# Half the gathered tokens in a PEER block: wider up products, high part first, gathers a batch ahead, GELU stores on ScalarE's queue

## What is computed

```python
q = (xt @ w_q).reshape(T, PEER_HEADS, 2, PEER_HALF)
s = jnp.einsum('thpc,hpnc->thpn', q, sub_keys)
s_top, i_top = lax.top_k(s, PEER_TOPK)
cand_s = s_top[:, :, 0, :, None] + s_top[:, :, 1, None, :]     # 16 x 16 sums
cand_i = i_top[:, :, 0, :, None] * N_KEYS + i_top[:, :, 1, None, :]
best_s, pos = lax.top_k(cand_s, PEER_TOPK)
idx = jnp.take_along_axis(cand_i, pos, axis=-1)
gate = jax.nn.softmax(best_s, axis=-1)
...
act = jax.nn.gelu(jnp.einsum('tkd,td->tk', u_tab[ib], xb), approximate=False)
return jnp.einsum('tk,tkd->td', act * gb, v_tab[ib])
```

## Time and profile before

| what | us |
|---|---|
| median of 3 runs | 1585.91 |
| lowest and highest run | 1579.07, 1590.8 |
| the profiled execution's own time | 1588.34 |
| its span, first to last instruction | 1586.6 |
| TensorE busy | 1471.9 |
| VectorE busy | 1274.1 |

### The profile page before, as it was taken

How to read it: one execution, slowest core, us unless ns; L and a number is a source line. 1 busy time by engine, 2 the same in 40 slices (tenths; PEclk the granted TensorE clock), 3 DMA queues, 4 the chain that set the end, 5 groups by cost and what they waited for, 6 DMA issues and landing times.

```text
span 1586.6 us, 25321 instructions
## 1 busy us (share of the span) xinstructions
PE 1471.9 (93%) x9438; PEld 1325.3 (84%) x9438; DVE 1274.1 (80%) x2444; ACT 824.7 (52%) x1571; POOL 506.2 (32%) x425
## 2 busy tenths in 40 slices
PE   7999799999989888888897888999989999999999
PEld 6898688789889888888897887889878888888887
DVE  4638787776798697877867876999989999999997
ACT  4553453151434656655665854554455556565553
POOL 4011620110466666656661111322322222222220
PEclk9999899999999999989999999999999999999999
DMA  6220004030465788887889998999899999999993
GB/s 201 81 81 1 8 29 162 28 125 35 143 209 181 270 289 285 282 269 259 286 285 394 369 353 307 379 379 372 328 414 410 410 410 409 407 411 405 409 401 124
DMA packets 168439, 420.49 MB, mean 265 GB/s; under 512 B 12896, under 2 KB 100096, under 8 KB 151680
## 3 DMA queue, kind: packets, MB, share of 16 engines
q1 hardware_dynamic: 140608, 251.10, 44.8%
q0 software_dynamic: 27712, 167.82, 27.1%
HBM read 372.44 MB, written 46.40 MB: 264 GB/s over the span
## 4 chain that ended last, share of the span: by engine, by line
PE 55%; DMA 7%; DVE 4%; issue 4%; POOL 3%; ACT 2%; SPq 1%; ACTq 0%; DVEq 0%
PE bank L2432 7%; PE bank L2434 7%; PE bank L2433 7%; PE bank L2108 5%; PE bank L2109 5%; PE bank L2110 5%; DMA early_gelus<-early_gelu 5%; PE bank L2127 4%; PE banks L2432 3%; PE banks L2434 3%; PE banks L2433 3%; POOL u_split L2008 2%; PE bank L2420 2%; PE bank L2421 2%; PE bank L2422 2%
## 5 line engine op out<-in xcount | busy, mean ns | idle before, releaser
L2108 PE MATMUL bank<-x_hi,u_split 128*128 128x320 f32 x832 | 268.7, 323 | 7.8 <-POOL u_split L2008 7.3
L2109 PE MATMUL bank<-x_lo,u_split 128*128 128x320 f32 x832 | 260.3, 313 | 0.0
L2110 PE MATMUL bank<-x_hi,u_split 128*128 128x320 f32 x832 | 259.8, 312 | 0.0
L1804 POOL DMA_INDIRECT scores<-in_peer_uv,pair_index x86 | 106.7, 1241 | 392.2 <-DVE pair_sum L1828 391.2
L2108 PEld LDWEIGHTS bank<-x_hi,u_split 128*128 128x128 f32 x832 | 160.7, 193 | 12.2 <-issue 9.8
L2479 ACT ACTIVATE act_tile<-onehots 128x384 f32<-128x384 f32 x128 | 124.3, 971 | 82.3 <-DVE act_lo L2521 76.9
L2127 PE MATMUL bank<-onehot_j,onehot_gated 128*128 128x128 f32 x768 | 109.2, 293 | 58.6 <-issue 42.0
L2109 PEld LDWEIGHTS bank<-x_lo,u_split 128*128 128x128 f32 x832 | 160.4, 193 | 0.0
L2110 PEld LDWEIGHTS bank<-x_hi,u_split 128*128 128x128 f32 x832 | 159.8, 192 | 0.0
L2127 PEld LDWEIGHTS bank<-onehot_j,onehot_gated 128*128 128x128 f32 x768 | 100.9, 204 | 65.8 <-issue 65.1
L2008 POOL TENSOR_TENSOR u_split<-u_raw,u_split 128x1024 fp32r<-128x1024 f32 x41 | 99.2, 2420 | 119.8 <-ACT u_split L2165 61.2
(11 more groups left out here) (433 smaller groups left out, 4037.0 us busy)
## 6 DMA issues: line engine op xcount, KB each, us to landing
v_raw<-in_peer_v SPq DMA_DIRECT2D x128, 512.0 KB, 10.7
u_raw<-in_peer_u SPq DMA_DIRECT2D x64, 512.0 KB, 5.5
u_raw_more<-in_peer_u SPq DMA_DIRECT2D x64, 512.0 KB, 4.9
gates<-gate_stage SPq DMA_DIRECT2D x24, 1024.0 KB, 11.6
onehots<-gates SPq DMA_DIRECT2D x32, 768.0 KB, 11.6
early_gelus<-early_gelu SPq DMA_DIRECT2D x104, 160.0 KB, 4.8
gelu_tile<-early_gelus SPq DMA_DIRECT2D x104, 160.0 KB, 11.3
w_raw<-in_w_in SPq DMA_DIRECT2D x9, 1024.0 KB, 5.0
```

Of the source, the lines that this page charges most:

```text
L1804: pool.indirect_dma_start(self.slot(k), None, self.table, bass.IndirectOffsetOnAxis(ap=self.sidx[:, k:k + 1], axis=0)).then_inc(self.lande ...
L2108: nc.tensor.matmul(out, uh[:, q, w], m.xh[:, k, P + NS:], start=(k == 0), stop=False)
L2109: nc.tensor.matmul(out, uh[:, q, w], m.xl[:, k, P + NS:], start=False, stop=False)
L2110: t = nc.tensor.matmul(out, ul[:, q, w], m.xh[:, k, P + NS:], start=False, stop=(k == KD - 1))
```

## The change

NS goes from 64 to 32, so TU from 320 to 352 columns, NR from 2 to 4, and the dots from 64 to 32. EARLY goes from 104 to 96, so iterations with an up product in the last stage from 24 to 32. With the new table ups_in, FIRST goes from 27 to 21; batches 0 to 31 hold 54 up products in place of 56 (10 batches with one, in place of 8), batches 32 to 47 hold 16 as before, and 5 follow. GpSimd fetches before the low parts, four rows in batch 0 and then two, so for the dots of the next batch. An up product waits for the high part, runs its 16 matmuls with it, and only then waits for the low part. ScalarE itself issues the GELU store, right behind the GELU, and waits for that GELU first. SyncE keeps the u loads (now 4 tiles ahead in its order, in place of 6) and the gate stores.

```diff
-EARLY = 104
+EARLY = 96
...
-NS = 64
+NS = 32
...
-    ups_in = [1 if n >= LATE or n % 4 == 3 else 2 for n in range(NB_)]
+    ups_in = [1 if n >= LATE or n % 3 == 2 else 2 for n in range(NB_)]
...
-                def store_gelu(n):
-                    banks.wait_taken(sp, ("up", n))
-                    sp.dma_start(gelus[n], ge[:, n % 2, 0:TU]).then_inc(nxt.ge_out[n % 2], 16)
-
...
                 for n in range(NB_):
                     for t in ups_of[n]:
-                        tile(t)
+                        load_u(t + NU)
                     if n % 2:
                         store_gates(n)
...
                 for n in range(LATE):
+                    for k in range(fetched, min(NS, fetched + (DOTS if n else 2 * DOTS))):
+                        up_rows.fetch(pool, k)
+                        fetched += 1
                     for t in ups_of[n]:
                         pool_low(t)
-                    for k in range(fetched, min(NS, fetched + DOTS)):
-                        up_rows.fetch(pool, k)
-                        fetched += 1
...
                     banks.wait_free(pe, g)
-                    wait_low(pe, n)
+                    pe.wait_ge(u_hi, n + 1)
                     q, out = n % 2, banks.bank(g)[:, 0:TU]
                     for k in range(KD):
                         w = slice(k * P, (k + 1) * P)
                         nc.tensor.matmul(out, uh[:, q, w], m.xh[:, k, P + NS:], start=(k == 0), stop=False)
                         nc.tensor.matmul(out, uh[:, q, w], m.xl[:, k, P + NS:], start=False, stop=False)
+                    wait_low(pe, n)
+                    for k in range(KD):
+                        w = slice(k * P, (k + 1) * P)
                         t = nc.tensor.matmul(out, ul[:, q, w], m.xh[:, k, P + NS:], start=False, stop=(k == KD - 1))
...
                     nc.scalar.activation(ge[:, n % 2, 0:TU], banks.bank(("up", n))[:, 0:TU],
                                          ACT.Gelu).then_inc(banks.taken["act"], 1)
+                    banks.wait_taken(act, ("up", n))
+                    act.dma_start(gelus[n], ge[:, n % 2, 0:TU]).then_inc(nxt.ge_out[n % 2], 16)
```

More of the change, by code:

```diff
@@ L2043, in store_gates @@
                                  stage[:, q].rearrange("p g t j -> p g (t j)")).then_inc(stored[q], 16)
-                def tile(n):
-                    if n + 6 < EARLY + NU:
-                        load_u(n + 6)
-                    store_gelu(n)
-                for n in range(2, 6):
+                for n in range(2, FIRST + NU):
                     load_u(n)
-                for n in range(FIRST):
-                    tile(n)
                 for n in range(NB_):
                     for t in ups_of[n]:
-                        tile(t)
+                        load_u(t + NU)
                     if n % 2:
@@ L2062, in _ @@
                             sp.dma_start(m.v_raw[i], v_rows[i]).then_inc(nxt.v_in[i], 16)
-                for n in range(EARLY - LAST, EARLY):
-                    tile(n)
+                for n in range(EARLY - LAST + NU, EARLY + NU):
+                    load_u(n)
                 for half in range(2):
```

## The result

| | us |
|---|---|
| before, median of 3 runs | 1585.91 (1579.07 to 1590.8) |
| changed, median of 3 runs | 1569.09 (1568.38 to 1569.77) |
| ratio, 95% interval | 0.9892 (0.9842 to 0.9941) |
| span of the changed kernel's profiled execution | 1567.4 |

The forecast was 1567, range 1550 to 1597. The change gains 1.1%, 16.8 us. By the prediction's stages the span moved from 1586.6 to 1567.4 so: A 14.7 shorter, B 43.4 shorter, C 3.7 shorter, D 42.6 longer.

A forecast was written before the change was run, and what follows sets the result against it. TensorE was taken as the bound in Stage D, with gather waits in Stage B and VectorE or bandwidth in Stage C. 901.9 + 665.9 = 1567.8 of span, plus 1.74 outside, less 2.43, gave 1567 us, range 1550 to 1597.

The forecast's parts named there:

- Stage A: Up products alone, to the first gate product's end: forecast to end at 509.3, where before it was 521.3.
- GpSimd's hold: Batch 0: four gathers, the fourth waiting for dot 3 at 503.5, delay a low part to 507.0.
- Stage B: Batches 0 to 31, 310.8 us before: forecast 259.6 of TensorE work plus 13 of gaps, ending at 781.9.
- 9 or 10 more: First 14 batches: VectorE 0.7 us a batch slower than TensorE, partly overlapping late low parts, 13 us in all.
- Stage C: Batches 32 to 47 and five last up products, 128.5 us before: forecast 120, bounds 112 and 130.
- Stage D: The last stage, bound by TensorE, 626.0 us before: forecast 39.9 longer, 665.9.
- The 1.5 us set aside for 1% more bytes: Last stage, iterations without an up product: 16 KB more GELU loads, between nothing and 3.5 us.
- The first: Rival: bandwidth holds batches 32 to 47 at 128.5 us, stores or u loads still waiting; 1582 us, chance 0.15.
- The second: Rival: gathers still late in 14 batches, low parts behind them, 28 to 32 us more; 1597 us, chance 0.08.
- The third: Rival: long DMA issues on ScalarE's queue hold its other work, 23.3 us; 1599 us, chance 0.10.
- The fourth: Rival, better: gaps in batches 0 to 31 near 3 us, the next stage near 113; 1551 us, chance 0.09.
- The 41 us of TensorE's work: Whole kernel: 352 columns in place of 320 make each of 128 up products 0.32 us longer.

The follow-up runs named there:

- e4: The changed kernel with GpSimd's gathers put back behind the low parts of their batch, two per batch: 1587.64 us.
- e8: The changed kernel with SyncE's u loads two tiles further ahead, so a load stands in front of its batch's gate store: 1565.68 us.
- e11: e9 with the GELU stores on ScalarE's queue and SyncE's u loads two tiles further ahead, so all three reorderings at 64 tokens: 1530.41 us.
- e2: The changed kernel with the GELU stores back on SyncE's queue and the u loads in their old order: 1577.53 us.
- e1: The changed kernel run again with no edit, as the standard for the runs beside it: 1569.28 us.
- e7: The kernel before with the GELU stores on ScalarE's queue and the u loads in the new order: 1598.82 us.
- e6: The kernel before (64 tokens, 104 early tiles) with the gathers a batch ahead, four in batch 0, and nothing else: 1560.62 us.
- e9: e6 with the high part first, GELU stores still on SyncE: 1546.12 us.
- e3: The changed kernel with each up product waiting for the low part before its first matmul: 1572.61 us.
- e10: The kernel before with the new numbers (32 tokens, 96 early tiles, new table) and the gathers ahead, low parts first, stores on SyncE: 1574.25 us.

## Why the prediction was right, point by point

**Stage A, GpSimd's hold at 509.3: right, but forecast 2.7 us too late.** (The prediction's own terms, 507.0 + 1.28 + 0.89, add up to 509.2.) The hold is where the prediction put it. "VectorE's selection does not change and delivers onehot_j at 507.0" is the part that failed: onehot_j was done at 501.9, dot 3 at 498.5 in place of 503.5. The likely reason was not in the account: VectorE stalls while GpSimd makes a low part (below), and in the changed kernel these stalls add up to some 8 us where before has 13. No run tried it apart. Half of the 5 us was lost again, since behind the 6.91 us of idle time the 8 low matmuls took 504.69 - 502.17 = 2.52 in place of 1.28, and gate product 1 1.91 in place of 0.89: the lower level of the clock, 1.2 GHz (mean granted clock 0.60 from 500 to 510 us).

**Stage B, 259.6 of work and 13 of gaps: right in kind, forecast 5.2 too long.** The gaps were 267.4 - 259.6 = 7.8, inside the bounds of 3 and 45. The low parts were priced right: two were expected late with some 5 us, three were, with 5.4. The term that failed is the "9 or 10 more" for VectorE. It was level, as the prediction has it, busy for 117.17 of the 118 us from 507 to 625, about the 14 batches with dots. But that is some 8.4 us a batch and not 8.8, TensorE's waits in that stretch are the 5.4 us for low parts alone, and behind it TensorE has none. e4 shows that the gathers' place in GpSimd's order carries the stage: 21.2 us of it.

**Stage C, 120: forecast 4.8 too short.** The term that failed is "A u load now stands right behind a gate store [...] so I give it nothing". Issues of 12.00 and 13.09 us made it 19.7 us of waits. e8 takes them away, and C gives back 1.9 to 2.8 of the 4.8, because the gate stores are late instead; with 64 tokens and the loads sooner C is 120.1 (e11). What was right: the stores' own waits went (41.1 to 2.6), at a price of 0.33 and 0.40 us of ScalarE's time per tile. e2 puts the stores' move, with the u loads' new place that goes with it, at 8.3 us, of which 4.2 in C; the stores alone are 11.9, of which 7.0 in C (e2 against e8).

The Trainium skill ("DMA: Bandwidth & Descriptors", section "Issuing engines are not separate DMA queues") holds that a second issuing engine saves only the sequencer's time to initiate the transfer, and that this is usually small beside the transfer. Taken as the prediction took it, C would have stayed at 128.5. It was 124.8, and 129.9 with the stores back on SyncE (e2), at DMA shares of 1.05 and 1.04. The measurement decides against that forecast. It bears the rule out in that the transfers themselves took nearly as long as before and what was saved was time ahead of the issue; but here that time was not small, 2.8 to 2.9 us a store in the median, beside some 7 us to landing. The rule that each DMA engine goes round its queues packet by packet (same page, "Queues, rings and completion order") is neither shown nor refuted: a store landed in 7.1 us from SyncE's queue and in 7.2 and 5.8 from ScalarE's.

**Stage D, 665.9: forecast 2.7 too short.** The 38.4 us of wider and more up products were right. The 1.5 us set aside for 1% more bytes was the wrong account of the 4.2 that followed. Counted by the starts of the down product's matmuls from 1250 to 1480 us, one comes every 0.2303 us in each of the nine kernels of 32 tokens and every 0.2287 in each of the five of 64, at a granted clock of 1.00. Over the 128 x 18 matmuls of the down products that is 3.7 us, an estimate that takes them all alike. The pause behind the last up products is 5.46 us in place of 4.43, another 1.0. Neither the DMA (e1's last stretch) nor the reorderings (every kernel of a width has the same pace) are why. The cause stays open; where the buffers lie in memory, which the width also moves, was not tried.

**The sum.** The errors, measured less forecast, are -2.7, -5.2, +4.8 and +2.7: 1567.8 of span against 1567.4. The total was better than its parts, and that is luck: two stages were forecast too long and two too short by nearly the same. The 2 us between 1567 and the measured median of 1569.09 come from taking off 2.43 for a profiled execution above its median; the changed kernel's profiled execution is its median.

**The rivals.** The first (bandwidth holds C) fell with 41.1 to 2.6 us of store waits, though its second half, the u loads behind the gate stores, took place. The second (gathers still late) fell: VectorE has no such wait in the list for B. The third (ScalarE held by its queue) fell as told: no issue of a GELU store there was over 0.35 us. But e7 shows a form of it that the prediction didn't have: not a long issue, but 0.75 us of ScalarE per tile, which fits a loss of up to 14 us when ScalarE lies on the path of B and none when it doesn't. The fourth (better) was met in B only.

**What the prediction didn't ask.** It weighed the change as one. Gathers ahead are 23.5 us alone (e6) and 18.4 in the whole (e4); stores on ScalarE's queue are a loss of 12 to 15 alone (e7) and a gain of 11.9 (e2 against e8) and 15.7 (e9 against e11) behind the gathers; the high part first is 14.5 at 64 tokens (e9) and 3.3 at 32, which is not clear of the noise (e3); the new numbers cost 3.2 alone, 13.6 behind the gathers (e10), and 35.3 behind all reorderings (e8 against e11). The 41 us of TensorE's work were right in the sum; that they bought waits which a reordering takes away for nothing was not looked at.

## What to carry to other kernels

A change that pays with work on the bound engine for fewer waits elsewhere should be priced against the kernel whose waits have first been taken away by reordering: here the trade was nearly even alone and cost 35 us afterwards. In an in-order queue, put what another engine needs a step later ahead of what waits, and then look who stands behind it. Take a combined change apart before keeping it whole, since the same step can lose 12 us or gain 12 by what else is in place.

## What the runs showed of the hardware

VectorE stood still while GpSimd worked. In before, two neighbouring instructions of VectorE on 128x128 values, and the low part that GpSimd ran meanwhile:

```profile
428.74 0.23 DVE L1455 CAST packed_words<-packed 128x128 uint32<-128x128 f32 x1
429.00 2.44 DVE L1456 TENSOR_SCALAR packed_low<-packed_words 128x128 uint32<-128x128 uint32 x1
```

```profile
428.94 2.42 POOL L2008 TENSOR_TENSOR u_split<-u_raw_more,u_split 128x1024 fp32r<-128x1024 f32 x1 [1.56 <-ACT u_split L2165]
```

The second starts 0.06 us after GpSimd's and ends 0.08 after it, at 2.44 us in place of the 0.23 of its neighbour. Before has five such places in stage A with some 13 us in all (the longest 4.94 us, against a pair of low parts), the changed kernel four with some 8; the MAX8 and FIND_INDEX8 instructions between them ran through low parts undisturbed. The Trainium skill ("SBUF — State Buffer", section "SBUF: two separate sides") calls the port pair that the two share an exclusive lock for a whole instruction, and the rows agree with it. Whether a small instruction meets a low part depends on a few tenths of a us, so a shift of anything ahead can move the selection by some 2.2 us at a time; no run tried this.

Three more are told above. A matmul of 512 columns came every 0.2303 us in the kernels of 32 tokens and every 0.2287 in those of 64 at the full granted clock, whatever the DMA share, with no cause found. The issue of a u load on SyncE's queue behind a 1024 KB gate store took 12 and 13 us, where the same kernel's issues on ScalarE's queue were never over 0.35. And a store written behind such an issue started 2.8 us late in the median in stage C of e2, though once issued it landed about as fast from either queue.
